# The router from unnormalised rows, and expert matrices loaded in runs of 8 KB, two experts to a transfer

## The reference

```python
    h = h + merged @ w_out[l]
    h = h + hier_moe(rms_norm(h, norm2_g[l]), w_router_group[l], b_router_group[l],
                     w_router_expert[l], b_router_expert[l], w_expert_in[l], w_expert_out[l])
...
def hier_moe(xn, w_group, b_group, w_er, b_er, w_e_in, w_e_out):
    g_logits = (xt @ w_group).astype(jnp.float32) + b_group.astype(jnp.float32)
    g_sel = jnp.argmax(g_logits, axis=-1)
    g_prob = jnp.take_along_axis(jax.nn.softmax(g_logits, axis=-1), g_sel[:, None], axis=1)
    e_logits = ((xt @ w_er).astype(jnp.float32) + b_er.astype(jnp.float32)).reshape(T, N_GROUPS, EXPERTS_PER_GROUP)
    e_in_group = jnp.take_along_axis(e_logits, g_sel[:, None, None], axis=1)[:, 0]
    top_v, top_i = lax.top_k(e_in_group, TOP_K_INNER)
    gates = g_prob * jax.nn.softmax(top_v, axis=-1)
...
    hdn = lax.ragged_dot(xs, w_e_in, group_sizes)
    gate_h, up_h = jnp.split(hdn, 2, axis=-1)
    act = jax.nn.silu(gate_h) * up_h
    ys = lax.ragged_dot(act, w_e_out, group_sizes)
```

## Time and profile before

| | |
|---|---|
| median of 3 runs | 1403.89 us (1403.79 to 1405.28) |
| profiled execution | 1404.4 us |
| its span | 1402.7 us |
| PE busy | 1240.2 us, 88% |
| POOL busy | 780.5 us, 56% |
| ACT / DVE busy | 629.3 us, 45% / 518.3 us, 37% |
| HBM read | 272.85 MB, 195 GB/s over the span |
| chain that ended last | PE 67%, ACT 9%, DMA 8%, DVE 7% |

### The profile page before, as it was taken

How to read it: one execution, slowest core, us unless ns; L and a number is a source line. 1 busy time by engine, 2 the same in 40 slices (tenths; PEclk the granted TensorE clock), 3 DMA queues, 4 the chain that set the end, 5 groups by cost and what they waited for, 6 DMA issues and landing times.

```text
span 1402.7 us, 19403 instructions
## 1 busy us (share of the span) xinstructions
PE 1240.2 (88%) x7815; PEld 1021.0 (73%) x7815; DVE 518.3 (37%) x1014; ACT 629.3 (45%) x1078; POOL 780.5 (56%) x347
## 2 busy tenths in 40 slices
PE   5999999895776767798889999999999889799997
PEld 4878877775422332477768999988998677799986
DVE  3728753533211211235642222202256381332211
ACT  4444533641110101454645655546689442655551
POOL 4779986440000000495107888878778904688884
PEclk9999999996899999999999999999999999899999
DMA  6455554285699999754004565455534422555552
GB/s 231 151 180 180 180 180 150 94 314 207 263 410 409 410 410 410 262 181 165 31 0 154 175 213 181 165 180 180 180 126 175 152 104 67 167 188 180 180 181 75
DMA packets 138333, 275.03 MB, mean 196 GB/s; under 512 B 7380, under 2 KB 53772, under 8 KB 138252
## 3 DMA queue, kind: packets, MB, share of 16 engines
q1 hardware_dynamic: 137980, 272.87, 54.0%
q10 hardware_dynamic: 272, 1.05, 0.2%
HBM read 272.85 MB, written 1.05 MB: 195 GB/s over the span
## 4 chain that ended last, share of the span: by engine, by line
PE 67%; ACT 9%; DMA 8%; DVE 7%; POOL 3%; issue 3%; SPq 2%; DVEq 0%; ACTq 0%
PE lin_ps L866 11%; PE lin_ps L867 11%; PE lin_ps L868 11%; PE lin_ps L886 6%; PE lin_ps L889 6%; PE lin_ps L888 6%; DMA ring<-in_w_expert_in 5%; POOL w_low L797 3%; ACT w_high L1370 3%; PE sc_ps L1112 3%; PE lin_ps L1098 2%; PE tr_ps L1136 1%; PE lin_ps L971 1%; PE sc_ps L940 1%; PE lin_ps L1127 1%
## 5 line engine op out<-in xcount | busy, mean ns | idle before, releaser
L797 POOL TENSOR_TENSOR w_low<-ring,w_high 128x1024 fp32r<-128x1024 f32 (+1 forms) x320 | 771.8, 2449 | 605.5 <-ACT w_high L1370 605.4
L1370 ACT ACTIVATE w_high<-ring 128x1024 fp32r<-128x1024 f32 (+1 forms) x320 | 311.9, 1040 | 139.0 <-PE lin_ps L868 88.3
L886 PE MATMUL lin_ps<-x_high,w_high 128*128 128x256 f32 x960 | 272.9, 284 | 1.7 <-DVEq L2128 1.7
L888 PE MATMUL lin_ps<-x_high,w_low 128*128 128x256 f32 x960 | 271.8, 283 | 0.0
L889 PE MATMUL lin_ps<-x_low,w_high 128*128 128x256 f32 x736 | 208.4, 283 | 0.0
L886 PEld LDWEIGHTS lin_ps<-x_high,w_high 128*128 128x128 f32 x960 | 184.5, 192 | 2.0 <-DVEq L2128 1.9
L888 PEld LDWEIGHTS lin_ps<-x_high,w_low 128*128 128x128 f32 x960 | 184.5, 192 | 0.1
L866 PE MATMUL lin_ps<-w_high,x_high 128*128 128x512 f32 (+1 forms) x432 | 170.6, 395 | 2.6 <-POOL w_low L797 2.6
L867 PE MATMUL lin_ps<-w_low,x_high 128*128 128x512 f32 (+1 forms) x432 | 168.6, 390 | 0.0
L868 PE MATMUL lin_ps<-w_high,x_low 128*128 128x512 f32 (+1 forms) x368 | 143.5, 390 | 0.0
L889 PEld LDWEIGHTS lin_ps<-x_low,w_high 128*128 128x128 f32 x736 | 141.4, 192 | 0.0
(11 more groups left out here) (377 smaller groups left out, 1930.7 us busy)
## 6 DMA issues: line engine op xcount, KB each, us to landing
ring<-in_w_expert_in SPq DMA_DIRECT2D x32, 2048.0 KB, 19.1
ring<-in_ffn_w_in SPq DMA_DIRECT2D x44, 1024.0 KB, 7.7
ring<-in_w_in SPq DMA_DIRECT2D x15, 2048.0 KB, 7.8
ring<-in_b_w_in SPq DMA_DIRECT2D x11, 2048.0 KB, 8.1
work<-in_w_expert_out SPq DMA_DIRECT2D x8, 2048.0 KB, 23.9
ring<-in_w_expert_out SPq DMA_DIRECT2D x8, 2048.0 KB, 23.2
ring<-in_ffn_w_out SPq DMA_DIRECT2D x8, 2048.0 KB, 7.9
ring<-in_w_mem_kv SPq DMA_DIRECT2D x4, 2048.0 KB, 11.7
```

The source lines that it names most:

```text
L797: pool.tensor_tensor(w_low[:, slot, 0:words], raw, w_high[:, slot, 0:words].bitcast(F32), ALU.subtract).then_inc(low_made, 1)
L886: pe.matmul(out, wh[:, j, at], high(k), start=(k == 0 and f < 2), stop=False, skip_group_check=True)
L888: pe.matmul(out, wl[:, j, at], high(k), start=False, stop=False, skip_group_check=True)
L1370: act.activation(w_high[:, slot, 0:words], raw, ACT.Copy).then_inc(high_made, 1)
```

## The change

It has two parts and a rearrangement that follows from them.

**Router from unnormalised rows.** Since the root of a row is one factor, the logits are computed as (h x gain) times the router matrix, and the factor is applied to the result. PE turns the first four parts of `h` inside w_out1, ahead of its part k = 2, and multiplies them ahead of k = 6. After w_out1, the other four parts follow. The sums of squares are taken in halves. `scaled`, which the gather needs, is now made by ACT, after its table load for Exp. Selection is made for both tiles at once and `sel` ahead of the gates. The first round stands outside the loop over rounds; the register load and a branch come after it.

**Expert matrices.** An input slot a (of two) holds four row groups of all four experts, so that each partition reads 8 KB in a row of an expert; an output slot holds both halves of the rows, again 8 KB in a row. A transfer brings two experts and has 2 MB as before. Two transfers fill a slot, both on the same semaphore, and PE gives a slot back after all of its matmuls: 4 `expert_used` semaphores instead of 8. The order of issue of batches 1 to 3 is as before; from batch 4 on the output matrices of a batch follow all of its input matrices.

```diff
-EXPERT_SLOTS = 8
+EXPERT_SLOTS = 4
...
-            def load_first(b, j):
-
-                src = io["w_expert_in"][0][bass.ds(b * BATCH, BATCH)].rearrange("e (p k) n -> p e k n", k=KC)
-                sp.dma_start(ring[:, j, :].rearrange("p (e k n) -> p e k n", k=2, e=BATCH), src[:, :, 2 * j:2 * j + 2, :])\
-                    .then_inc(expert_in[j], 16)
...
+            def load_first(b, a, pair_of_experts):
+
+                e0 = 2 * pair_of_experts
+                src = io["w_expert_in"][0][bass.ds(b * BATCH + e0, 2)].rearrange("e (p k) n -> p e k n", k=KC)
+                sp.dma_start(first_slot(a)[:, e0:e0 + 2], src[:, :, 4 * a:4 * a + 4, :]).then_inc(expert_in[a], 16)
+
+            def load_second(b, parity, pair_of_experts):
+
+                src = io["w_expert_out"][0][bass.ds(b * BATCH + 2 * pair_of_experts, 2)].rearrange("e (p f) n -> p e f n", f=2)
+                sp.dma_start(second_slot(parity, pair_of_experts), src).then_inc(expert_in[2 + parity], 16)
...
                 with sp.Fori(2, BATCHES // 2) as pair:
                     for parity in range(2):
-                        for j in range(3):
-                            first_when_free(pair, parity, j)
-                        second_when_free(pair, parity, 0)
-                        first_when_free(pair, parity, 3)
-                        second_when_free(pair, parity, 1)
+                        for a in range(2):
+                            firsts_when_free(2 * pair + parity, 2 * pair + parity, a)
+                        seconds_when_free(pair, 2 * pair + parity, parity)
...
+            def first_half_of_router(k):
+                if k == 2:
+                    pe.wait_ge(h_half, TILES)
+                    turn("moe", KC // 2, both(h))
+                if k == 6:
+                    tr_wait(pe, "moe", KC // 2)
+                    pe.wait_ge(router_in, 32)
+                    pe.wait_ge(lin_moved[blocks["router"][0] % 2], blocks["router"][0] // 2)
+                    router_products(0, KC // 2)
+
+            linear("w_out1", *parts(merged_high, merged_low), ready=first_half_of_router)
...
+            pe.wait_ge(h_half, 2 * TILES)
+            for k in range(KC // 2, KC):
+                for c0, view in both(h)(k):
+                    mm = pe.transpose(split_ps(k)[:, c0:c0 + P], view, ident[:])
+                mm.then_inc(h_turned, 1)
+            for k in range(KC // 2, KC):
+                pe.wait_ge(h_taken, k - KC // 2 + 1)
+                mm = router_products(k, 1)
             mm.then_inc(router_used, 1)
...
-                        for j in range(4):
-                            pe.wait_ge(expert_in[j], 16 * it + 16)
...
+                        for a in range(2):
+                            pe.wait_ge(expert_in[a], 32 * it + 32)
+                            for k in range(4):
                                 for e in range(BATCH):
...
+                            mm.then_inc(expert_used[a], 1)
...
+            expert_round(0)
+            pe.wait_ge(router_done, 1)
+            n_rounds = pe.value_load(rounds[0:1, 0:1], min_val=1, max_val=SEQ // CAP)
+            with pe.If(n_rounds > 1):
+                with pe.Fori(1, n_rounds) as r:
+                    expert_round(r)
...
+            step(act.activation(small[:, 60:61], eps[:], ACT.Exp))
+            act.wait_ge(h_root, 1)
+            for t in range(TILES):
+                ins = act.activation(scaled[:, t, :].rearrange("p (k f) -> p k f", k=KC),
+                                     h[:, t, :].rearrange("p (f k) -> p k f", k=KC), ACT.Copy, scale=small[:, 6 + t:7 + t])
+            ins.then_inc(normed, 1)
             act.wait_ge(router_group, 1)
...
+            for k in range(KC // 2, KC):
+                dve.wait_ge(h_turned, k - KC // 2 + 1)
+                dve.tensor_scalar(xT[:, k, :], split_ps(k), col("norm2", k), None, ALU.mult).then_inc(h_taken, 1)
+            dve.wait_ge(norm_std, 3 * TILES)
+            dve.reciprocal(small[:, 6:8], small[:, 2:4]).then_inc(h_root, 1)
+            dve.wait_ge(h_root, 1)
```

More of the change, by code:

```diff
@@ L132, in weight_block @@
             for w, c0, n in sources:
-                order = "(p k) n -> p k n" if name == "router" else "(k p) n -> p k n"
-                loads.append((kn, width, at, n, w[k0 * P:(k0 + kn) * P, c0:c0 + n].rearrange(order, p=P)))
+                loads.append((kn, width, at, n, w[k0 * P:(k0 + kn) * P, c0:c0 + n].rearrange("(k p) n -> p k n", p=P)))
                 at += n
```

239 lines of the change are left out of this document (125 added, 114 removed).

## The result

The changed kernel takes 1392.29 us (median of 5 runs, 1391.93 to 1395.83), the kernel before 1403.79 (5 runs, 1399.51 to 1405.28). The ratio is 0.9932 with a 95% interval of 0.9916 to 0.9948. The forecast was 1390.3 us with a range of 1383 to 1399. The profiled execution took 1391.93 us, its span is 1390.2 us, 12.5 us less than the 1402.7 before.

What follows compares the result with a forecast made beforehand. The expert stage was taken as bound by its weight loads, the DMA engines being full. Terms -10.45 - 5.8 + 1.7 + 1.0 = -13.55 us gave 1390.8 for the profiled execution, 1390.3 for the median; range 1383 to 1399.

Steps and rivals of the forecast that it cites:

- Start of the stream: Expert loads on SP's queue: first reload at 351.2 instead of 361.62, so the stream starts 10.45 us earlier.
- w_out1's end: Router transposes and products inserted into w_out1 on PE make it end 3.05 us later, at 326.2.
- Add to logits: Router after w_out1: adds, second half's transposes and products, logits at 330.6; 4.4 us.
- Logits to counts: Selection on DVE, from the logits to the selection sum ahead of the count matmuls: 4.7 us, at 335.3.
- Counts to pick: Count matmuls, small DVE operations ending 0.2 us later, rounds and loop entry; first pick at 339.55, 4.25 us.
- First pick to first L1125: Gather and first hidden-layer matmuls follow the first pick as before, 7.8 us, at 347.3.
- The rival that the router's gain is half lost: Inserted transposes wait in w_out1 and the clock is low; stream only 5 to 6 us earlier, 1395; chance 0.12.
- Tightest point: Stream of loads: first load of batch 4 leaves 1 to 2 us before the queue empties; gap at most 2 us.
- a DMA share below 1 inside the stage: Sign of error in the middle of the expert stage: release by halves starves the stream of loads.
- Run length: Expert loads in 8 KB runs go at 422 GB/s, 4.97 us per load; forty loads save 5.8 us.
- Low clock in the last matmuls: PE's last 32 output matmuls, after some 5 us idle, run slower: 1.7 us added.
- End of the stage: Register load and branch between last batch and norm delay DVE and ACT's square: 1.0 us added, bounds -1 and +4.

Runs made afterwards that it cites:

- x_loads: Kernel before with only the expert-load half (8 KB runs, two experts per transfer, release by halves); router and loop over rounds as before: 1403.48 us, ratio 1.0007.
- x_nobranch: Changed kernel without the branch over the second-round loop, and that loop, on PE alone; register load kept: 1393.91 us (1 run).
- after: The changed kernel itself, first set of runs and first trace, against the kernel before: 1392.29 us, ratio 0.9932.
- after_again: The changed kernel unaltered, measured once more (the second set of runs and second trace): 1396.78 us, ratio 0.9946 against the kernel before.
- x_runs4k: Changed kernel with loads from the first reload on in runs of 4 KB, a quarter of all four experts per transfer: 1398.40 us.
- x_runs16k: Changed kernel with each input-matrix transfer bringing one whole expert in runs of 16 KB; computation differs from the reference: 1389.36 us (1 run).
- x_loop: Changed kernel with PE and ACT entering the loop over rounds with round 0 inside, as before; DVE keeps register load and branch: 1391.12 us.

## Why the prediction was right, and where its terms were off

**Start of the stream.** Predicted 10.45 us earlier, measured 12.1 (a + b of 43.53 against 55.64) in the first trace and 8.8 in the second. Point by point: w_out1's end, 3.05 us later predicted, is 2.5 later; the insertions cost 3.7, but the clock was better than before by 1.1. Add to logits 4.4 predicted and measured. Logits to counts 4.7 predicted, 4.84 measured. Counts to pick 4.25 predicted, 3.64 measured: here the small operations on DVE were predicted to end 0.2 us after PE's count matmuls, and it was the other way round (L2083 waits 0.20 us for PE). First pick to first L1125 7.8 predicted, 7.25 measured. The first reload came 3.69 us after the first L1125 (3.9 in the sum). The rival that the router's gain is half lost did not happen.

**Tightest point.** I had placed it at the first load of batch 4, and the first hole is there, of some 0.5 us. A second one, of about 1 us, follows at the first load of batch 5, which I had held safe. The sum had nothing for a hole, and its text at most 2 us; the estimate above gives 1.4 us in this trace and 3.6 in x_loads. The sign that I had named for it, a DMA share below 1 inside the stage, did show (0.94 at 460 to 465).

**Run length.** 5.8 us predicted, 4.8 measured. The straight line through 2 and 4 KB gave the rate that was measured, 422 GB/s, and a run of 8 KB did go as one packet: the queue has 125,692 packets where it had 137,980, 256 fewer for each of the 48 loads. What is short is c: its 4.8 us are 0.12 us a load or, at 16 runs per engine, 7.5 ns per run instead of 9.4, and by the estimate above the holes account for about what is missing. The Trainium skill, DMA: Bandwidth & Descriptors, section Why small descriptors are slow, has about 3 cycles per packet, which by the working ahead of the result is 2.2 us for the forty loads; the runs show at least twice that.

**Low clock in the last matmuls.** 1.7 us predicted, 1.68 measured (d, 10.14 to 11.82). The wait ahead of them was 3.22 us where some 5 were predicted.

**End of the stage.** 1.0 us predicted with bounds of -1 and +4, measured 5.0, outside of them, and 3.3 in the second trace. This is the term that was mis-sized. I had put it on DVE, with the register load of 0.78 us; DVE's path from the shift of the places to ACT's square grew only from 2.4 to 3.0 us (566.23 to 569.24). The loss is on PE, 3.2 us of branch (0 in x_nobranch), and then a low clock in the first products of the memory block, which no step of mine had. I had named the branch, but as a bound only, and on another engine; that its target has to be fetched is not shown. The sign that I had named for it, more than 5 us from the shift of places to ACT's square, did not show: it looked at the wrong engine.

**Sum.** -13.55 predicted, of which -10.4 came in the stage; 1.2 us of the kernel's 12.5 were there before the change begins and 0.9 after it. The profiled execution took 1391.93 us against 1390.8 of the sum. The end of the stage cost 4.0 more than I had put down, the stream was 0.8 longer, and the start (1.7), the head (1.2) and the rest (0.9) made up for most of it: +1.1. So the forecast owes its closeness in part to luck: errors of 4.8 us one way met 3.8 us the other way, of which 2.1 lie outside of the change. The second set of runs lies 6.5 us above the forecast, of which 2.8 are the low clock in a.

## What to carry to other kernels

When a stream of transfers bounds a stage, price an edit by when the first free slot is given back and by the length of the stream; everything else in the stage is hidden. Then ask who stands at the join behind the stage: an If over a long body on the engine that has to start next cost about 2 us of the path and up to 3 more for the clock behind it, against 4.8 that the longer runs gave; a loop entered ahead of the stage cost 0.9. A last transfer should be small for its consumer, and work that fills an engine's known wait can be worth more than the same work put into a busy stretch (1.4 us in a, of which 0.75 were left at the first reload). And count the loads that lie queued at each release: with slots given back in halves and the new order, holes of 1 to 5 us in all opened in the stream.

## What the runs showed of the hardware

- A branch that skips a loop's body held PE for 2.7 to 3.2 us in the four traces that have it (after 3.22, after_again 2.66, x_runs4k 3.05, x_runs16k 2.98), with a register load of no visible cost. The Trainium skill, Advanced Engine Details and Errata, section Control Flow Timing, gives about 108 ns for a compare-and-branch; the branch here does not agree with it. That the time is a fetch of instructions is likely, since in all four traces one packet of the instruction queue comes within 0.5 us of the gap's start and a second one some 0.5 us behind its end (565.5 and 568.75 us in the changed kernel), while x_loop has none there and x_nobranch one, but these runs don't show it.
- The rate of full transfers rose with the run up to 16 KB: 410, 422 and 427 GB/s over the same 60 us. Each run went as one packet: x_runs16k has 121,596 packets, 128 fewer than the changed kernel for each of its 32 input loads. What beyond a fixed part per run makes 16 KB gain 3 us stays open.
- The granted clock fell to 0.5 (1.2 GHz) in w_out1 in some executions and not in others of the same kernel, at 308 to 316 us, after two idle times of 1.1 us each on PE. It is worth up to 2.8 us, more than most edits tried here.
- Where sixteen of the last output matmuls ran 2.1 to 3.3 us ahead of the others (five traces), both halves took 1.92 us; 32 that waited 2.9 to 4.3 us for the last transfer took 5.06 to 5.34 us, and in one trace, after a wait of 2.41 us, 6.48.
